# Part of a down product is moved behind the start of a mixer, and queries and key scores are made in two halves

## The chip, the cores and the metric

The kernel runs on one core of a Trainium2 chip, in f32. The metric is the device time of one execution, in microseconds; 2289.24 is the median of three (2287.36 to 2290.9).

## What is computed

256 tokens of width 1024 go through a first block (modulated SwiGLU, a mixer of sparse attention and a recurrent branch, a second SwiGLU) and then through two hybrid layers. Only these matter here:

```python
# first block, second SwiGLU
y = swiglu(h, ffn2_w_gate[l], ffn2_w_up[l], ffn2_w_down[l])       # down: 2816 -> 1024
x = x + 0.5 * m[8][:, None, :] * rmsnorm(y, ffn2_post_g[l])
# each of two hybrid layers
u = rms_norm(x, attn_norm_w) @ w_in                               # HGRN, attention, SSM
x = x + mix @ w_out
# expert layer, for each block of 128 tokens
q = (xt @ w_query).reshape(T, H, 2, PEER_HALF)                    # H = 8 heads
s = jnp.einsum('thcd,cnd->thcn', q, sub_keys)                     # 128 keys a side
sv, si = lax.top_k(s, K)                                          # K = 16
top_s, pos = lax.top_k(cand_s, K); idx = jnp.take_along_axis(cand_i, pos, axis=-1)
a = jnp.einsum('thkd,td->thk', down[ib], xb)
c = gate * jax.nn.gelu(a)
out = jnp.einsum('thk,thkd->td', c, up[ib])
```

## The kernel before

Tokens are handled in two blocks of 128 (tb 0 and 1). All dense weights are stored as 1 MB tiles (128 x 2048) and pass through a ring of four slots; SyncE issues their loads in the order of the list `STREAM` (L72), each as soon as the tile four places before it has been used (`tiles_used`, L1092). The wait for a tile and the release of its slot are part of the product that uses it.

The second SwiGLU of the first block ends with the down product `down(1, tb, 0, 11)` (L1406, L1397): 11 tiles for each token block, four products of 128 x 512 a tile, summed in PSUM banks 4 and 5 for block 0 and 6 and 7 for block 1. Its tiles are loaded once for each block. `post(2, tb)` closes it: ScalarE takes the mean square and the root (L1125 to L1128), VectorE the reciprocal, scales (L1614) and adds to x (L1615).

Then come four mixers, `i` = 0 to 3 (two layers, two token blocks). A mixer is three generators, one for each of ScalarE (L285), TensorE (L446) and VectorE (L700), whose `yield`s number its steps. `Beside(...).to(k)` runs the steps up to k. Mixer 0 runs alone, all steps in a row. Mixers 1 to 3 run beside the experts of the token block before: step k of TensorE after pick k of 128, those of the two others at slots of the same count. Steps touched by the change or the prediction:

- step 4: transposes of the normalized x (L452), copied and scaled by ScalarE (L308); steps 8 to 48: the input product (`weights`, L458), with the recurrence levels between
- step 57: logits; 58: the SSM product (L637), behind VectorE's L868; 61, 62: transposed probabilities (L617); 64, 65: values (L624)
- 68: transposes of the mix, 71 to 78: output product; 84: transposes of htok; 87 to 94: queries in two chunks (four parts each); 95, 97: transposes of the queries; 101, 103: key scores (L696), copied by ScalarE at L433, L437 and L443

The experts follow (`picks_*`, L909 to L1085). Per unit of one head, VectorE searches the 16 best keys on each side, their 16 best pairs and the indices (`search`, steps 0 to 6); it waits for both halves of the scores first. GpSimd gathers 16 pairs of rows for each token, one pick (8 KB a token, 1 MB in all) at a time, into a ring of eight slots of `wide` (L1060), slot k again once TensorE has used pick k - 8. VectorE makes dot products two picks at a time (L1011), ScalarE the gelu (L925) and the diagonals (L930), TensorE the weighted sum in banks 6 and 7 (L944). The first index of mixer 0's scores starts the first gather.

SBUF is laid out twice in the same bytes: `one` for the first block, `two` for the layers. In `one`, `actT` (the input of the down product), `rows` and `xn` lie at the front, where `wide` lies in `two`.

```python
            for tb in range(TB):
                down(1, tb, 0, 11)
            pe.wait_ge(m["smalls2_loaded"], 32)
            Beside(mixer_tensor(pe, 0, tile)).to(LAST)
            for i in range(MIXERS - 1):
                picks_tensor(pe, i, Beside(mixer_tensor(pe, i + 1, tile)))
            picks_tensor(pe, MIXERS - 1)
```

## Time and profile before

| | |
|---|---|
| median of three runs | 2289.24 us |
| profiled execution | 2289.02 us, span from the first to the last instruction 2287.3 |
| TensorE busy | 1992.7 us, 87% of the span, mean granted clock 0.963 |
| VectorE / ScalarE / GpSimd busy | 57% / 27% / 27% |
| bytes | 796.41 MB, mean 348 GB/s |
| gathers | 574.65 MB, 61.5% of the 16 DMA engines' span |
| weight tiles and other loads by sequencer | 209.73 MB, 24.5% |

Busy shares are means over the whole span. The span has two parts: up to about 800 us dense products (the first block, and mixer 0 alone), then the expert stage. A chain of waits follows the work that ended last back from the end; idle time in brackets stands before an instruction, with what ended it.

### The profile page before, as it was taken

To read this page: it belongs to the slowest core of one execution; us is meant where nothing else is said; L and a number is where in the kernel's file an instruction comes from. 1 tells how busy PE (TensorE), PEld (TensorE's weight loads), DVE (VectorE), ACT (ScalarE), POOL (GpSimd) and SP (SyncE) were. 2 spreads that over 40 slices of the span, in tenths; PEclk is the share of its full clock that TensorE was granted. 3 is DMA by queue.
4 is the path that set the end of the run, shared out by engine and by line. 5 is a ranking of instruction groups with operands and counts; after the bars stand their busy time and mean duration, and the time that the engine had idled before them with its cause. 6 is when DMAs were issued, how large, how long until landed. Compare 5 with 4: busy or idle time off the path is not lost.

```text
span 2287.3 us, 20001 instructions
## 1 busy us (share of the span) xinstructions
PE 1992.7 (87%) x6128; PEld 1070.0 (47%) x6128; DVE 1295.1 (57%) x3368; ACT 620.1 (27%) x1510; POOL 611.9 (27%) x554
## 2 busy tenths in 40 slices
PE   3999999899998769989979898977999898777776
PEld 2886577588644334444424443433444443333332
DVE  5550155200015276776577778658687767777764
ACT  2000125200013232453223245223225332222221
POOL 1100000000000043334333333334333334454442
PEclk8999999999999879999999999999999999999999
DMA  9987943444685499999999999999999999999997
GB/s 389 390 341 271 316 148 137 167 157 154 236 299 210 147 379 421 421 383 403 421 417 405 421 421 388 422 422 405 419 420 419 360 399 416 403 422 420 421 417 324
DMA packets 113380, 796.41 MB, mean 348 GB/s; under 512 B 12377, under 2 KB 15961, under 8 KB 17416
## 3 DMA queue, kind: packets, MB, share of 16 engines
q0 software_dynamic: 78912, 574.65, 61.5%
q1 hardware_dynamic: 28944, 209.73, 24.5%
q10 hardware_dynamic: 5432, 10.93, 1.3%
q8 instruction: 42, 0.69, 0.1%
q14 instruction: 50, 0.41, 0.0%
HBM read 794.19 MB, written 4.75 MB: 349 GB/s over the span
## 4 chain that ended last, share of the span: by engine, by line
PE 56%; DMA 22%; DVE 11%; ACT 5%; issue 4%; POOL 1%; POOLq 0%; DVEq 0%; ACTq 0%
DMA wide<-experts_in,pick_idx 21%; PE PS L944 17%; PE PS L1351 17%; PE PS L458 10%; PE PS L1401 8%; DVE wide L1011 4%; ACT diag L930 1%; POOL wide L1060 1%; DMA ring<-wts_in 1%; DMA early<-ada_in 1%; DVE topi L962 1%; DVE topi L959 1%; ACT L925 1%; DVE topf L961 1%; PE PS L696 1%
## 5 line engine op out<-in xcount | busy, mean ns | idle before, releaser
L944 PE MATMUL PS<-wide,diag 128*128 128x512 f32 x2048 | 994.4, 624 | 225.2 <-ACT diag L930 219.4
L1060 POOL DMA_INDIRECT wide<-experts_in,pick_idx x512 | 584.7, 1142 | 1326.3 <-PE PS L944 796.3
L1011 DVE CUSTOM_DVE_ANT_0 wide<-wide,htok 128x1024 f32<-128x1024 f32 x512 | 619.9, 1225 | 278.0 <-DMA wide<-experts_in,pick_idx 271.2
L944 PEld LDWEIGHTS PS<-wide,diag 128*128 128x128 f32 x2048 | 386.1, 197 | 751.5 <-issue 409.2
L1351 PE MATMUL PS<-hT,ring 128*128 128x256 f32 x1744 | 382.7, 382 | 15.2 <-DMA ring<-wts_in 11.6
L1351 PEld LDWEIGHTS PS<-hT,ring 128*128 128x128 f32 x1744 | 333.5, 192 | 64.5 <-issue 16.7
L458 PE MATMUL PS<-ring,hTm 128*128 128x512 f32 (+1 forms) x704 | 324.4, 591 | 2.1 <-ACT hTm L308 1.7
L930 ACT ACTIVATE diag<-cst,coef 128x128 f32<-128x128 f32 x512 | 177.6, 394 | 275.9 <-DVE coef L1022 273.4
L925 ACT ACTIVATE coef<-dots 128x2 f32<-128x2 f32 x256 | 52.3, 204 | 639.8 <-DVE dots L1011 639.3
L458 PEld LDWEIGHTS PS<-ring,hTm 128*128 128x128 f32 x704 | 134.5, 193 | 164.8 <-issue 155.5
L1401 PE MATMUL PS<-ring,actT 128*128 128x512 f32 x352 | 153.8, 598 | 2.0 <-DMA ring<-wts_in 2.0
L1636 DVE TENSOR_TENSOR actT<-silu,PS 128x256 f32<-128x256 f32 (+1 forms) x44 | 18.5, 421 | 231.8 <-ACT silu L1188 231.8
L1401 PEld LDWEIGHTS PS<-ring,actT 128*128 128x128 f32 x352 | 67.2, 192 | 86.1 <-issue 82.4
L1188 ACT ACTIVATE silu<-PS 128x256 f32<-128x256 f32 x44 | 16.9, 384 | 290.4 <-PE PS L1351 290.4
L1629 DVE CUSTOM_DVE_ANT_0 early<-early,cact 128x1024 f32<-128x1024 f32 x72 | 84.2, 1219 | 14.2 <-DMA early<-ada_in 14.1
L1612 DVE RECIPROCAL stat<-stat 128x1 f32<-128x1 f32 x6 | 1.0, 164 | 140.0 <-ACT stat L1128 140.0
L1022 DVE TENSOR_TENSOR coef<-coef,gate 128x2 f32<-128x2 f32 x256 | 41.2, 161 | 61.7 <-ACT coef L925 56.7
L925 ACT ACT_TABLE_LOAD x58 | 74.4, 1283 | 1.0
L1116 POOL TENSOR_TENSOR bias_t<-bias_t,early 128x1024 f32<-128x1024 f32 (+1 forms) x2 | 7.9, 3930 | 192.4 <-DVE early L1731 192.4
L1109 POOL DMA_DIRECT2D early<-ada_in x32 | 16.9, 528 | 132.4 <-DVE modr L1629 132.4
L1011 DVE DVE_READ_ACCUMULATOR2_ANT dots<- 128x1 f32 x512 | 41.9, 82 | 0.0
L913 ACT ACT_TABLE_LOAD x31 | 39.8, 1283 | 0.5
(316 smaller groups left out, 1241.0 us busy)
## 6 DMA issues: line engine op xcount, KB each, us to landing
ring<-wts_in SPq DMA_DIRECT2D x199, 1024.0 KB, 5.7
early<-ada_in POOLq DMA_DIRECT2D x36, 1024.0 KB, 8.5
wide<-experts_in,pick_idx POOLq DMA_INDIRECT x512, 12.4
strip_t<-strips_one ACTq DMA_DIRECT2D x1, 2048.0 KB, 12.0
strip_dil<-strips_one ACTq DMA_DIRECT2D x1, 1536.0 KB, 19.0
x<-x_in ACTq DMA_DIRECT2D x1, 1024.0 KB, 9.0
bias_t<-strip_t ACTq DMA_DIRECT2D x1, 1024.0 KB, 13.8
wrow<-norm_row_in ACTq DMA_DIRECT2D x2, 512.0 KB, 6.5
```

What stands on the lines that cost most here:

```text
L458: last = pe.matmul(PS[:, c % 2, 0:n], hTm[:, k, :], w[:, k % 4 * BANK:k % 4 * BANK + n], start=k == 0, stop=k == 7, skip_group_check=True)
L696: last = pe.matmul(PS[:, G2 + h // 2, (h % 2) * 256:(h % 2 + 1) * 256], qT[:, h * P:(h + 1) * P], o2(l, "keys", 0, 256), start=True, stop= ...
L913: act.activation(topf[:, 128 + 32 * (u % 2):144 + 32 * (u % 2)], topf[:, 112 + 32 * (u % 2):128 + 32 * (u % 2)], ACT.Exp).then_inc(m["gate ...
L925: act.activation(coef[:, 0, rr % 2, :], dots[:, rr % 2, :], ACT.Gelu_apprx_tanh).then_inc(m["gelu_ready"], 1)
L930: act.activation(diag[:, (rr * ROUND + j) % RING, :], ident, ACT.Copy, scale=coef[:, 1, rr % 2, j:j + 1])\
L944: last = pe.matmul(PS[:, ACC + half, :], diag[:, n % RING, :], ups[:, n % RING, half * BANK:(half + 1) * BANK], start=k == 0, stop=k == PI ...
L1011: v.tensor_tensor_reduce(out=downs[:, n % RING, :], in0=downs[:, n % RING, :], in1=htok[:, tb, :], scale=1.0, scalar=0.0, op0=ALU.mult, op ...
L1022: v.tensor_tensor(coef[:, 1, rr % 2, :], coef[:, 0, rr % 2, :], gate[:, u % 4, rr * ROUND:(rr + 1) * ROUND], ALU.mult)\
L1060: pool.indirect_dma_start(pairs_of_rows[:, k % RING, :, :].rearrange("p c n -> p (c n)"), None, experts.rearrange("l e d -> (l e) d"), bas ...
L1351: last = pe.matmul(outp, a, b, start=i == 0, stop=i == len(pairs) - 1)
L1401: last = pe.matmul(PS[:, bank + half, :], src[:, 2 * t + k, tb * P:(tb + 1) * P], w[:, k * D + half * BANK:k * D + (half + 1) * BANK], sta ...
L1629: v.tensor_tensor_reduce(out=w, in0=w, in1=cact[:, :], scale=1.0, scalar=0.0, op0=ALU.mult, op1=ALU.add, accum_out=modr[:, 8 * j + n:8 * j ...
```

## The change

The down product of token block 1 is no longer one piece. Three of its 11 tiles are used right behind token block 0's product; one (the fourth) after step 57 of mixer 0, the two halves of the fifth after steps 62 and 65, the sixth after step 82, and five behind the mixer's last step. `STREAM` has the tiles in the new order; their number is the same. `actT` now lies under the last three gather slots, so GpSimd waits before gather 5 of the first unit until the last of these tiles has been used. `post(2, 1)` is called in the experts of block 0, on ScalarE ahead of the first gelu, on VectorE after the first two dot products; it writes to `lgt` and `htok[:, 1]` in place of `junk` and `xn`. TensorE waits for it ahead of the first expert product.

In every mixer the second query chunk is split around the first chunk's transposes and key scores, scores of heads 0 to 3 go to banks 4 and 5 and those of heads 4 to 7 to banks 2 and 3, ScalarE's copies follow that order, and VectorE waits for the first half ahead of head 0 and for the second ahead of head 4. The arguments `beside=None, opening=None` are added to `picks_scalar` and `picks_vector`.

```diff
@@ -71,14 +71,17 @@
-          ("out1", "out1", [0, 1, 0, 1, 2, 3, 2, 3]), ("gu2", "gu2", range(FT)), ("dn2", "dn2", [*range(FT // 2)] * TB)]
-for _i in range(MIXERS):
+          ("out1", "out1", [0, 1, 0, 1, 2, 3, 2, 3]), ("gu2", "gu2", range(FT)), ("dn2", "dn2", range(FT // 2)),
+          ("late0", "dn2", range(0, 3)), ("in_0", "in_0", range(14)), ("late1", "dn2", range(3, 5)), ("out_0", "out_0", range(4)),
+          ("late2", "dn2", range(5, 6)), ("query_0", "query_0", range(4)), ("late3", "dn2", range(6, FT // 2))]
+for _i in range(1, MIXERS):
...
+LATE = [FIRST[f"late{_p}"] + _t for _p, _c in enumerate((3, 2, 1, 5)) for _t in range(_c)]
@@ -159,8 +162,7 @@
-        actT = sb("actT", [P, FT, S], stack=one)
-        rows = sb("rows", [P, 3, D], stack=one)
+        row1 = sb("row1", [P, D], stack=one)
@@ -181,10 +183,15 @@
+        used = D + 2 * D + KC * S + 4 * S + W1 + WC1 + 16 * 3 + 8 + 72 * 2 + 24 * 2 + 16 + 8 + 32
+        sb("low_rest", [P, RING * 2 * D - 3 * 2 * D - used], stack=one)
+        actT = sb("actT", [P, FT, S], stack=one)
+        sb("high_rest", [P, 3 * 2 * D - FT * S], stack=one)
...
+        row0 = sb("row0", [P, D], stack=one)
+        cact = sb("cact", [P, D], stack=one)
...
-        cact = sb("cact", [P, D], stack=one)
@@ -203,6 +210,7 @@
+        rows = [row0[:, :], row1[:, :], htok[:, 1, :]]
@@ -428,19 +436,17 @@
             for c in range(2):
-                yield 92 + 4 * c
+                yield 92 + 10 * c
                 act.wait_ge(m["tiles_used"], FIRST[f"query_{i}"] + 2 * c + 2)
                 act.copy(u[:, c * BANK:(c + 1) * BANK], PS[:, c, :]).then_inc(m["q_copied"], 1)
-            yield 99
-            for b in (0, 1):
-                act.wait_ge(m["q_T"], 2 * i + b + 1)
-                act.copy(u[:, D + b * BANK:D + (b + 1) * BANK], PS[:, G2 + b, :]).then_inc(m["qT_copied"], 1)
-            for b in (0, 1):
-                yield 104 + b
-                act.wait_ge(m["scores_ready"], 2 * i + b + 1)
+                yield 96 + 10 * c
+                act.wait_ge(m["q_T"], 2 * i + c + 1)
+                act.copy(u[:, D + c * BANK:D + (c + 1) * BANK], PS[:, G2 + c, :]).then_inc(m["qT_copied"], 1)
+                yield 100 + 10 * c
+                act.wait_ge(m["scores_ready"], 2 * i + c + 1)
                 if i:
                     act.wait_ge(m["topk_ready"], EXPERT_HEADS * i)
-                act.copy(key_scores.rearrange("p h c n -> p (h c n)")[:, b * D:(b + 1) * D], flat(PS[:, G2 + 2 * b:G2 + 2 * b + 2, :]))\
+                act.copy(key_scores.rearrange("p h c n -> p (h c n)")[:, c * D:(c + 1) * D], flat(PS[:, 4 - 2 * c:6 - 2 * c, :]))\
                     .then_inc(m["s_copied"], 1)
@@ -681,21 +687,35 @@
             weights("query", 0, 3)
-            for part in range(4):
-                yield 91 + part
-                weights("query", 1, part)
-            for c in range(2):
-                yield 95 + 2 * c
+            qT = u[:, D:2 * D]
+
+            def query_turn(c):
                 pe.wait_ge(m["q_copied"], 2 * i + c + 1)
                 turn(G2 + c, u[:, c * BANK:(c + 1) * BANK], 4).then_inc(m["q_T"], 1)
-            qT = u[:, D:2 * D]
-            for b in (0, 1):
-                yield 101 + 2 * b
-                pe.wait_ge(m["qT_copied"], 2 * i + 2)
+
+            def keys(b):
+                pe.wait_ge(m["qT_copied"], 2 * i + b + 1)
                 for h in range(4 * b, 4 * b + 4):
-                    last = pe.matmul(PS[:, G2 + h // 2, (h % 2) * 256:(h % 2 + 1) * 256], qT[:, h * P:(h + 1) * P],
+                    last = pe.matmul(PS[:, 4 - 2 * b + (h - 4 * b) // 2, (h % 2) * 256:(h % 2 + 1) * 256], qT[:, h * P:(h + 1) * P],
                                      o2(l, "keys", 0, 256), start=True, stop=True)
                 last.then_inc(m["scores_ready"], 1)
+
+            yield 91
+            weights("query", 1, 0)
+            yield 94
+            query_turn(0)
+            yield 95
+            weights("query", 1, 1)
+            yield 98
+            keys(0)
+            yield 99
+            weights("query", 1, 2)
+            yield 100
+            weights("query", 1, 3)
+            yield 104
+            query_turn(1)
+            yield 107
+            keys(1)
@@ -919,6 +939,8 @@
+                if u == 0:
+                    opening()
@@ -964,8 +986,8 @@
                 if step == 0:
-                    if h == 0:
-                        v.wait_ge(m["s_copied"], 2 * (g // EXPERT_HEADS) + 2)
+                    if h % 4 == 0:
+                        v.wait_ge(m["s_copied"], 2 * (g // EXPERT_HEADS) + 1 + h // 4)
                     best16(best[:, 0:16], besti[:, 0:16], key_scores[:, h, 0, :])
@@ -1036,6 +1058,8 @@
+                    if u == rr == 0:
+                        opening()
@@ -1070,6 +1094,8 @@
                         pool.wait_ge(m["ups_used"], u * K16 + k - RING + 1)
+                    if opening and k == RING - 3:
+                        pool.wait_ge(m["tiles_used"], LATE[-1] + 1)
                     pool.sem_inc(m["gather_starts"], 1)
@@ -1122,8 +1148,8 @@
-            def mean_square(src, n, col, width, done):
-                act.activation(junk[:, 0:n], src, ACT.Square, accum_out=stat[:, col:col + 1]).then_inc(m["sq_done"], 1)
+            def mean_square(src, n, col, width, done, out=junk):
+                act.activation(out[:, 0:n], src, ACT.Square, accum_out=stat[:, col:col + 1]).then_inc(m["sq_done"], 1)
@@ -1135,7 +1161,8 @@
                 act.wait_ge(m["tiles_used"], done)
-                mean_square(flat(PS[:, bank:bank + 2, :]), D, 12 + 4 * i + 2 * tb, D, "y_root_fb")
+                mean_square(flat(PS[:, bank:bank + 2, :]), D, 12 + 4 * i + 2 * tb, D, "y_root_fb",
+                            flat(lgt) if i == 2 and tb else junk)
@@ -1148,7 +1175,7 @@
-                act.copy(rows[:, i, :], flat(PS[:, bank:bank + 2, :])).then_inc(m["rows_ready"], 1)
+                act.copy(rows[i], flat(PS[:, bank:bank + 2, :])).then_inc(m["rows_ready"], 1)
@@ -1329,12 +1356,9 @@
-            first = Beside(mixer_scalar(act, 0))
-            first.to(1)
-            post(2, 1, FIRST["dn2"] + 22, 6)
-            first.to(LAST)
+            Beside(mixer_scalar(act, 0)).to(LAST)
...
-                picks_scalar(act, i, Beside(mixer_scalar(act, i + 1)))
+                picks_scalar(act, i, Beside(mixer_scalar(act, i + 1)), lambda: post(2, 1, LATE[-1] + 1, 6))
@@ -1587,10 +1611,33 @@
             pe.wait_ge(m["rows_ready"], 3)
-            for tb in range(TB):
-                down(1, tb, 0, 11)
+            down(1, 0, 0, 11)
+
+            def late(t, halves=(0, 1)):
+                w = tile(LATE[t])
+                for k in halves:
+                    for half in range(2):
+                        last = pe.matmul(PS[:, 6 + half, :], actT[:, 2 * t + k, P:S], w[:, k * D + half * BANK:k * D + (half + 1) * BANK],
+                                         start=t == k == 0, stop=t == 10 and k == 1, skip_group_check=True)
+                if 1 in halves:
+                    last.then_inc(m["tiles_used"], 1)
+
+            for t in range(3):
+                late(t)
             pe.wait_ge(m["smalls2_loaded"], 32)
-            Beside(mixer_tensor(pe, 0, tile)).to(LAST)
+            first = Beside(mixer_tensor(pe, 0, tile))
+            first.to(57)
+            late(3)
+            first.to(62)
+            late(4, (0,))
+            first.to(65)
+            late(4, (1,))
+            first.to(82)
+            late(5)
+            first.to(LAST)
+            for t in range(6, 11):
+                late(t)
+            pe.wait_ge(m["x_ready"], 6)
             for i in range(MIXERS - 1):
@@ -1611,8 +1658,9 @@
-                V(v.scalar_tensor_tensor(xn[:, tb, :], flat(PS[:, bank:bank + 2, :]), r, rows[:, i, :], ALU.mult, ALU.mult))
-                v.tensor_tensor(x[:, tb, :], x[:, tb, :], xn[:, tb, :], ALU.add).then_inc(m["x_ready"], 1)
+                y = rows[2] if i == 2 and tb else xn[:, tb, :]
+                V(v.scalar_tensor_tensor(y, flat(PS[:, bank:bank + 2, :]), r, rows[i], ALU.mult, ALU.mult))
+                v.tensor_tensor(x[:, tb, :], x[:, tb, :], y, ALU.add).then_inc(m["x_ready"], 1)
@@ -1806,12 +1854,9 @@
-            first = Beside(mixer_vector(v, V, 0))
-            first.to(3)
-            post(2, 1, 6)
-            first.to(LAST)
+            Beside(mixer_vector(v, V, 0)).to(LAST)
...
-                picks_vector(v, V, i, Beside(mixer_vector(v, V, i + 1)))
+                picks_vector(v, V, i, Beside(mixer_vector(v, V, i + 1)), lambda: post(2, 1, 6))
```

## Rows read from the trace of the kernel before

**Rows 1.** The page, section 2: GB/s of DMA in 40 slices of 57.2 us.

```profile
GB/s 389 390 341 271 316 148 137 167 157 154 236 299 210 147 379 421 421 383 403 421 417 405 421 421 388 422 422 405 419 420 419 360 399 416 403 422 420 421 417 324
```

**Rows 2.** Stretches: us, engines busy (instructions), PEclk, DMA share, GB/s.

```profile
806.00:814.00 8.00, 0.00 (x0) 0.00 (x0) 6.49 (x21) 1.70 (x3) 5.87 (x6) 0.50 0.98 378
820.00:2260.00 1440.00, 1245.16 (x3208) 550.49 (x3207) 1029.57 (x2743) 469.30 (x1172) 574.66 (x502) 0.97 1.00 412
840.00:870.00 30.00, 30.00 (x80) 13.53 (x79) 17.13 (x42) 10.53 (x22) 8.91 (x9) 0.99 1.02 423
```

**Rows 3.** Chain that ended last: start us, us, what.

```profile
594.44 75.55 PE PS L1401 x176
```

**Rows 4.** Timeline of TensorE: start us, us, line op, tiles, count [idle before].

```profile
669.81 1.04 PE L452 MATMUL PS<-cst,mx 128*128 128x128 f32 x8
672.54 12.28 PE L458 MATMUL PS<-ring,hTm 128*128 128x512 f32 x28 [1.69 <-ACT hTm L308]
...
723.54 1.00 PE L570 MATMUL PS<-i_tok,u 128*128 128x64 f32 x8
...
737.10 2.82 PE L637 MATMUL PS<-xdt,u 128*128 128x64 f32 x12 [3.13 <-DVE u L868]
...
744.08 1.97 PE L624 MATMUL PS<-v_tok,hTm 128*128 128x64 f32 x8 [2.16 <-ACT hTm L410]
...
747.85 1.97 PE L452 MATMUL PS<-cst,mx 128*128 128x128 f32 x8 [0.94 <-DVE mx L895]
750.19 14.84 PE L458 MATMUL PS<-ring,hTm 128*128 128x512 f32 x32 [0.38 <-ACT hTm L418]
768.91 1.94 PE L452 MATMUL PS<-cst,htok 128*128 128x128 f32 x8 [3.88 <-DVE htok L906]
770.72 14.80 PE L458 MATMUL PS<-ring,hTm 128*128 128x512 f32 x32
...
787.53 3.73 PE L696 MATMUL PS<-s,u 128*128 128x256 f32 x16 [0.68 <-ACT u L437]
815.64 11.09 PE L944 MATMUL PS<-wide,diag 128*128 128x512 f32 x20 [24.38 <-ACT diag L930]
```

**Rows 5.** Stretches of the first mixer and its clock; columns as in rows 2.

```profile
735.00:751.00 16.00, 9.94 (x39) 8.27 (x40) 5.00 (x15) 8.52 (x32) 0.00 (x0) 0.50 0.00 1
753.00:768.00 15.00, 12.03 (x29) 4.99 (x27) 1.97 (x4) 1.44 (x3) 0.00 (x0) 1.00 0.74 247
769.00:772.00 3.00, 3.00 (x10) 2.24 (x11) 0.00 (x0) 1.17 (x2) 0.00 (x0) 0.50 0.05 22
```

**Rows 6.** Timeline of ScalarE, the norm of block 0 and two copies.

```profile
632.25 1.02 ACT L1126 ACTIVATE silu<-PS 128x1024 f32<-128x1024 f32 x1 [37.38 <-PE PS L1401]
...
633.38 1.28 ACT L1128 ACT_TABLE_LOAD   x1
634.67 0.29 ACT L1128 ACTIVATE stat<-stat,cst 128x1 f32<-128x1 f32 x1
...
778.69 0.59 ACT L433 COPY u<-PS 128x512 f32<-128x512 f32 x1 [7.22 <-PE PS L458]
...
791.29 1.01 ACT L443 COPY key_scores<-PS 128x1024 f32<-128x1024 f32 x1 [0.72 <-PE PS L696]
```

**Rows 7.** Timeline of VectorE, the norm's rest, mx, the first search step.

```profile
635.20 1.28 DVE L1614 SCALAR_TENSOR_TENSOR xn<-PS,stat,rows 128x1024 f32<-128x1024 f32 x1
636.52 1.23 DVE L1615 TENSOR_TENSOR x<-x,xn 128x1024 f32<-128x1024 f32 x1
...
640.17 0.75 DVE L715 TENSOR_SCALAR mx<-x,mst 128x1024 f32<-128x1024 f32 x1 [0.25 <-DVE mst L714]
...
792.34 0.29 DVE L958 MAX8 topf<-key_scores 128x8 f32<-128x128 f32 x1 [23.48 <-ACT key_scores L443]
```

**Rows 8.** Timeline of GpSimd: the first gather issued.

```profile
803.43 0.99 POOL L1060 DMA_INDIRECT wide<-experts_in,pick_idx  x1 [450.10 <-DVE pick_idx L997]
```

**Rows 9.** Who line 443 (score copies, four mixers) waited for: us, times.

```profile
  PE PS L696: 4.5, 4
```

More of the change, by code:

```diff
@@ L907, in mixer_vector, with picks_scalar @@
                 .then_inc(m["h_ready"], 1)
-        def picks_scalar(act, i, beside=None):
+        def picks_scalar(act, i, beside=None, opening=None):
             def exps(u):
@@ L948, in picks_tensor, with picks_vector @@
                     beside.to(k)
-        def picks_vector(v, V, i, beside=None):
+        def picks_vector(v, V, i, beside=None, opening=None):
             iota = C("iota")
```

## The prediction

> **What bounds the kernel now.** I read the page's slices first. The bytes moved per second are low in slices 11 to 14 (572 to 800 us) and at a plateau from slice 16 on, with a few dips [rows 1]. The stretches behind it say the same: from 820 to 2260 us the DMA share is 1.00 at 412 GB/s [rows 2]. So the expert stage is a stage of bytes: 512 gathers of 1 MB, and the weight tiles of three more mixers beside them. At the 421 GB/s of its undisturbed slices a tile or a gather (128 x 2048 x 4 B) takes 2.49 us. What is done before the first gather has no such cover: it is one chain through TensorE and the small steps between engines. A microsecond taken out of it moves the whole expert stage forward, and a megabyte that is pushed behind the first gather costs 2.49 us again. The chain of waits puts the whole second-block down product on it: 176 matmul instructions in 75.55 us, 0.429 us each [rows 3]. A tile is eight instructions (two products of two halves, and one f32 matmul shows as two), so 3.43 us. The first token block's product ends at 594.44 + 88 x 0.429 = 632.2 us, the second's at 670.0. Then the first mixer runs alone, with TensorE waiting at four places near its end [rows 4], and from 791.3 to 815.6 us TensorE has nothing at all [rows 4].
>
> **1. Eight of eleven tiles leave the front.** Three stay ahead of the mixer: 632.2 + 24 x 0.429 = 642.5 us, where the mixer's first transposes stood at 669.8 [rows 4]. Their input, the normalized x of token block 0, is there earlier: VectorE has written mx by 640.9 [rows 7]. The loads hide: these are the same 22 tile loads in another order, the ring is fed four tiles ahead, and no idle stretch of TensorE in the down product or in the mixer names the ring. **-27.5 us.**
>
> **2. The closing norm of block 1 leaves the mixer's beginning.** ScalarE ran its square and root there ahead of the scaled copies of the transposes, and TensorE sat idle for 1.69 us [rows 4]. Without it the first copy starts behind the first four transposes (half of 1.04 us), about 0.9 us sooner. **-0.9 us.** The norm runs later instead (6).
>
> **3. Tiles put into the mixer.** Each costs what it is longer than the wait that it fills, at full clock: a tile of 3.43 us into 3.13 us (before L637), +0.3; half a tile of 1.72 into 2.16 (before L624), 0; half a tile into 0.94 (before the mix transposes), +0.8; a tile of 3.43 into 3.88 (before the htok transposes), 0 [rows 4]. **+1.1 us.** If a cover is shorter by the time it is reached, the difference is added, at most 3.4 us for a tile.
>
> **4. The clock.** TensorE is at 0.50 from 735 to 751 us and from 769 to 772 us, both times after such a wait, and at 1.00 between [rows 5]. The work on the chain in these stretches is slow: twelve 64-column instructions of L637 take 2.82 us where eight of the same form take 1.00 us at full clock, those of L624 2.97, the two groups of eight transposes 1.97 and 1.94 where the first group takes 1.04, and the 32 weight products behind each 14.84 and 14.80 where 32 x 0.429 is 13.7 [rows 4]. Were all of it at full clock, the chain would shorten by 1.4 + 1.4 + 0.5 + 1.1 + 0.5 + 0.9 = 5.8 us. The change puts dense matmuls into just these waits, but ScalarE and VectorE steps still leave TensorE partly idle between 738 and 748, so I take most of it, **-4.5 us**, with bounds 0 and -5.8, and a worse case in the rivals. The Trainium skill ("TensorE: Matmul & The Clock Gate", Part 1) says that the throttled state is the default and that activity releases it. By that rule an inserted tile can also begin throttled. Rows 5 agree with the rule, and show no inserted tile.
>
> Steps 1 to 4: **-31.8 us** for the end of the first query chunk, which ScalarE copied at 778.69 [rows 6].
>
> **5. Queries and keys in halves.** Now the search starts at 792.34, 13.65 us behind that copy, after the second chunk (6.9 us), both turns, all keys (3.73) and both score copies [rows 4, 6, 7]. In the new order it needs one query part (1.72, covering the 0.59 copy), one turn (0.5), a second part (1.72, covering the next copy), half the keys (1.87), one score copy (1.01), and some 0.3 of handing over: 7.1 us. **-6.6 us**, so the search begins 38.4 us earlier. The index search for head 0 stays as it is, so the first gather is issued 11.1 us behind that start, as now [rows 7, 8]. The new wait of VectorE, for the second half of the scores at head 4, is hidden by two units of expert work.
>
> **6. What is late next.** The DMA engines start on gathers some 2 us behind the first issue [rows 8], so at 766.8 instead of 805.2. But before, the ring had been filled with four tiles of the next mixer by then. Now five late tiles of the down product stand between, so these four loads are released one by one as the late tiles are used, beside the first gathers: 4 x 2.49 = **+10.0 us** of bytes. It would be free only if the stage had slack in its bytes, and from 840 to 870 us it has none, at 423 GB/s [rows 2]. The ramp that the first gathers show now, 378 GB/s for 8 us instead of 421, is filled by the tiles: **-0.8 us** [rows 2]. The new wait of GpSimd, before gather 5, ends with the last late tile. That is at 778.7 - 31.8 + 12.9 (three query parts, two turns, the keys and their copies) + 17.2 (five tiles) = 777.0 us. Gathers 5 to 15 and all later ones are queued behind it. The queue doesn't run dry: nine megabytes (gathers 0 to 4 and four tiles) last until about 789.
>
> The deferred norm waits for the same tile. Behind it on ScalarE stand the gelu and the diagonals of expert 0, on VectorE the weighing of round 0, and TensorE waits for its sum because banks 6 and 7 are shared. By its rows: square and its read 1.2, table load 1.28, root 0.29, reciprocal 0.16, scale 1.28, add 1.23, and handing over, 5.9 us, so x is ready at 782.9 [rows 6, 7]. A search step and the weighing follow, and the first expert product starts at about 785.1, against 815.64 [rows 4]: -30.5. So TensorE would allow 30.5, the bytes 38.4 - 10.0 + 0.8 = 29.2. The smaller one counts.
>
> **7. Later mixers.** The same reordering stands in mixers 1 to 3, beside picks. I cost it at nothing: bytes bound there, and the score copies waited for the keys by 4.5 us over all four mixers [rows 9]. If that cover goes, each mixer loses some of it; bounds -1 and +3 us for the three.
>
> **Sum.** -27.5 - 0.9 + 1.1 - 4.5 - 6.6 + 10.0 - 0.8 = **-29.2 us**. The profiled execution took 2289.02 (span 2287.3), 0.2 below the median of 2289.24; so 2259.8, rounded **2260 us**. Its own range, by the bounds of 4 and 7 and some 2 us for the queues of 6: 2254 to 2267.
>
> **Rivals.**
> *Throttled insertions.* The tiles in the waits run at 1.2 GHz, 6.9 us a tile, and lengthen what they were to fill. For: 0.50 stands in rows 5 in exactly these waits. Against: the clock was still 1.00 when the first wait began, and it came back soon in the dense products behind it. Price: no clock gain (+4.5), first tile +3.4, halves of the second +1.3 and +1.7: 10.9 us, so 2271.
> *The tile bytes cost nothing.* If the expert stage at its beginning is paced by TensorE and not by bytes (it is busy all through 840 to 870 us [rows 2], with expert products and mixer weights), and the deferred norm is quicker than I think, up to the whole head start stays: 2289.0 - 38.4 = 2251.
> *Slower.* In mixers 1 to 3 ScalarE now stops for TensorE at slots 101, 107 and 111, ahead of the gelus in its queue. If TensorE lags two picks with mixer work (2 x 3.43 = 6.9 us) at two more of these stops, with nothing queued to cover them, three mixers lose 41 us: 2301. It decides from 29.2 / 3 = 9.7 us a mixer on. Against: 4.5 us in all now [rows 9], and eight gathers in the ring.
> *It doesn't do what it says.* The gate before gather 5 leaves DMA dry for what was won: within 5 us of 2289. It would take 29 dry us, where I count nine megabytes queued.
>
> **How the numbers follow.** Forecast 0.64; throttled insertions 0.15; bytes for nothing 0.15; slower 0.04; no effect 0.02. To hold 8 in 10 the range takes the forecast's own, the throttled case at 2271 and most of the way to 2251: 2251 to 2271. Faster by over 0.2% (4.6 us, about what a measurement of this kernel can tell from no change) 0.94, within 0.02, slower 0.04.
>
> **What would show it.** In the changed profile: mixer transposes at 642.5; first search step near 754 and first gather issued near 765; last late tile near 777; first expert product near 785; granted clock above 0.50 in most of 707 to 720 (the former 735 to 751); DMA at the plateau from 768 on, without a gap near 790; the expert stage from the first gather to the end longer by about 9 us. A search start later than 760 makes the first steps wrong; a first product before 785 with an end later than 2265 makes 7 wrong; an end below 2254 makes the price of the four tiles wrong.

## The result and the profile after

The changed kernel took 2257.61 us in the median of four runs (2253.47 to 2260.71), against 2290.07 for the kernel before: a ratio of 0.9859 with a 95% interval of 0.9836 to 0.9881, 32.5 us less (27 to 38). The forecast was 2260. The profiled execution took 2254.79 us, its span 2253.1. It was already 2.2 us ahead at the end of block 0's down product (ScalarE's square begins at 630.05, in rows 6 at 632.25), which nothing in the change touches. So I count all that follows from that square, in every profile.

The slices of bytes after, of the same page section as rows 1: slice 14 (a slice is 56.3 us now) has 310 in place of 147, and the plateau is as before.

```profile
GB/s 389 381 353 262 316 171 150 164 153 149 218 283 217 310 421 421 421 367 422 422 419 421 416 422 382 422 421 390 422 409 411 370 414 419 417 421 418 412 412 331
```

The chain that ended last, from the down product to the first expert product (start us, us, what):

```profile
592.25 37.77 PE PS L1425 x88
630.01 10.30 PE PS L1620 x24
640.79 1.15 ACT hTm L316 x4
641.98 12.28 PE PS L464 x28
...
703.41 3.63 PE PS L1620 x8
707.04 1.30 PE PS L643 x12
...
712.48 1.55 PE PS L630 x12
714.03 1.77 PE PS L1620 x4
...
717.47 14.02 PE PS L464 x32
...
735.35 1.09 PE PS L458 x8
...
756.87 17.18 PE PS L1620 x40
774.07 1.11 ACT lgt L1152 x2
...
777.02 1.29 DVE htok L1662
778.34 1.23 DVE x L1663
781.58 6.38 PE PS L966 x8
```

Read beside rows 3 and 4: 24 late instructions stand ahead of the mixer instead of 88; ScalarE's copies follow the first transposes at once, without the square and root between; the tile at 703.41 fills the former 3.13 us, and the twelve instructions behind it (L643, formerly L637) take 1.30 us of the chain. In the timeline, the view of rows 4, they take 1.45, where rows 4 have 2.82. Clock and bytes in stretches like those of rows 2 and 5 (us, engines busy, PEclk, DMA share, GB/s):

```profile
705.00:721.00 16.00, 13.62 (x59) 7.84 (x58) 5.00 (x15) 8.12 (x30) 0.00 (x0) 1.00 0.39 133
722.00:738.00 16.00, 15.27 (x42) 6.92 (x41) 2.82 (x4) 2.52 (x5) 0.00 (x0) 1.00 0.88 303
763.00:796.00 33.00, 24.13 (x56) 10.60 (x55) 20.46 (x51) 10.78 (x20) 11.18 (x12) 0.84 1.01 419
```

The clock is 1.00 where it was 0.50, and the DMA engines are full from the first gathers on. ScalarE's copy of the first query chunk, VectorE's first search step, and GpSimd's gathers 0, 4, 5 and 8:

```profile
743.87 0.58 ACT L441 COPY u<-PS 128x512 f32<-128x512 f32 x1 [6.75 <-PE PS L464]
```

```profile
750.51 0.29 DVE L980 MAX8 topf<-key_scores 128x8 f32<-128x128 f32 x1 [15.22 <-ACT key_scores L449]
```

```profile
761.61 0.99 POOL L1084 DMA_INDIRECT wide<-experts_in,pick_idx  x1 [407.52 <-DVE pick_idx L1019]
...
766.64 0.94 POOL L1084 DMA_INDIRECT wide<-experts_in,pick_idx  x1 [0.30 <-issue]
774.85 0.94 POOL L1084 DMA_INDIRECT wide<-experts_in,pick_idx  x1 [7.27 <-PE PS L1620]
...
786.14 0.99 POOL L1084 DMA_INDIRECT wide<-experts_in,pick_idx  x1 [7.88 <-PE PS L966]
```

Gather 5 waits 7.27 us for the last late tile, gather 8 for the first expert product. In the window from 763 to 796 neither shows in the DMA share.

**The head start along the experts.** Each profile has 512 dot products of VectorE (L1011 before, L1033 after). The table is the start of dot product k, less the start of the square named above, minus the same in the kernel before; so it is the head start in us at that point, and the last column that at the end of the span. For instance k = 8, after and before: 798.01 - 630.05 and 829.89 - 632.25, so -29.7.

```profile
798.01 1.23 DVE L1033 CUSTOM_DVE_ANT_0 wide<-wide,htok 128x1024 f32<-128x1024 f32 x1 [0.50 <-DMA wide<-experts_in,pick_idx]
```

```profile
829.89 1.23 DVE L1011 CUSTOM_DVE_ANT_0 wide<-wide,htok 128x1024 f32<-128x1024 f32 x1 [0.52 <-DMA wide<-experts_in,pick_idx]
```

| profile | first search step | first expert product | k = 8 | 56 | 128 | 352 | 416 | end |
|---|---|---|---|---|---|---|---|---|
| changed kernel | -39.6 | -31.9 | -29.7 | -30.4 | -30.5 | -28.3 | -32.2 | -32.0 |
| again (e5) | -39.6 | -31.9 | -29.3 | -29.7 | -27.7 | -26.7 | -29.9 | -29.6 |
| a third time (e12) | -39.6 | -31.9 | -30.0 | -29.9 | -29.4 | -29.1 | -33.6 | -33.6 |
| e1, halves only | -7.2 | -7.0 | -7.0 | -7.7 | -6.6 | -8.0 | -12.7 | -12.5 |
| e2, move only | -32.6 | -27.4 | -28.7 | -28.8 | -27.4 | -27.7 | -28.1 | -28.2 |
| e3, five tiles without bytes | -39.6 | -31.9 | -35.0 | -33.9 | -30.4 | -32.3 | -36.1 | -36.1 |
| e4, two tile-times more | -39.6 | -25.0 | -28.1 | -27.8 | -26.6 | -27.8 | -30.9 | -31.0 |
| e10, four tile-times more | -39.6 | -18.1 | -21.3 | -21.3 | -22.1 | -21.2 | -24.6 | -24.6 |
| e6, halves in mixer 0 only | -39.6 | -31.9 | -29.6 | -30.3 | -27.5 | -27.3 | -27.7 | -27.6 |
| e7, inserts ahead | -24.5 | -16.7 | -14.8 | -15.1 | -13.6 | -15.2 | -17.9 | -17.9 |
| e8, inserts behind | -34.8 | -13.3 | -15.7 | -16.5 | -15.7 | -14.3 | -18.0 | -18.1 |
| e9, six tiles | -39.6 | -36.3 | -38.6 | -39.7 | -37.8 | -40.2 | -43.2 | -44.1 |
| e11, finer pieces | -40.5 | -34.0 | -34.2 | -34.2 | -31.5 | -31.2 | -35.4 | -35.1 |

Up to the first expert product the same kernel gives the same number to 0.1 us. Beside the experts it doesn't: three profiles of the changed kernel lie 2.8 apart at 128 and 4.0 at the end. Its 13 timed runs of all groups go from 2251.75 to 2262.62, median 2258.44, and the runs of the kernel before from 2282.43 to 2291.68. The table's first two columns are therefore firm, and a difference of less than some 3 us further right isn't, by one profile.

### The profile page after: what moved, and what is told of

It reads as the page before. It is cut to its first block, busy times and chain, and to the rows that moved or that the text cites. A ratio compares the mean times of both kernels' runs of the same rounds, so it can differ in the third digit from the quotient of the medians.

```text
span 2253.1 us, 20003 instructions
## 1 busy us (share of the span) xinstructions
PE 1997.4 (89%) x6128; PEld 1071.9 (48%) x6128; DVE 1294.5 (57%) x3368; ACT 621.3 (28%) x1511; POOL 623.2 (28%) x554
## 4 chain that ended last, share of the span: by engine, by line
PE 54%; DMA 25%; DVE 11%; ACT 4%; issue 4%; POOL 2%; POOLq 0%; DVEq 0%; ACTq 0%
DMA wide<-experts_in,pick_idx 23%; PE PS L1375 17%; PE PS L966 16%; PE PS L464 10%; PE PS L1425 6%; DVE wide L1033 4%; POOL wide L1084 2%; PE PS L1620 1%; ACT diag L952 1%; DMA ring<-wts_in 1%; DMA early<-ada_in 1%; DVE topi L981 1%; DVE topi L984 1%; PE PS L477 1%; PE PS L1464 1%
## 5 line engine op out<-in xcount | busy, mean ns | idle before, releaser
L966 PE MATMUL PS<-wide,diag 128*128 128x512 f32 x2048 | 1004.6, 630 | 194.2 <-ACT diag L952 188.6
L1084 POOL DMA_INDIRECT wide<-experts_in,pick_idx x512 | 595.9, 1164 | 1280.1 <-PE PS L966 780.3
L1033 DVE CUSTOM_DVE_ANT_0 wide<-wide,htok 128x1024 f32<-128x1024 f32 x512 | 619.8, 1224 | 285.4 <-DMA wide<-experts_in,pick_idx 279.3
L966 PEld LDWEIGHTS PS<-wide,diag 128*128 128x128 f32 x2048 | 390.9, 199 | 723.3 <-issue 425.0
L1425 PE MATMUL PS<-ring,actT 128*128 128x512 f32 x264 | 115.9, 600 | 2.0 <-DMA ring<-wts_in 2.0
L1425 PEld LDWEIGHTS PS<-ring,actT 128*128 128x128 f32 x264 | 50.4, 192 | 64.9 <-issue 61.3
L1033 DVE DVE_READ_ACCUMULATOR2_ANT dots<- 128x1 f32 x512 | 42.1, 82 | 0.0
## 6 DMA issues: line engine op xcount, KB each, us to landing
bias_t<-strip_t ACTq DMA_DIRECT2D x1, 1024.0 KB, 13.6
```

The lines of the kernel that those rows point to most:

```text
L966: last = pe.matmul(PS[:, ACC + half, :], diag[:, n % RING, :], ups[:, n % RING, half * BANK:(half + 1) * BANK], start=k == 0, stop=k == PI ...
L1033: v.tensor_tensor_reduce(out=downs[:, n % RING, :], in0=downs[:, n % RING, :], in1=htok[:, tb, :], scale=1.0, scalar=0.0, op0=ALU.mult, op ...
L1084: pool.indirect_dma_start(pairs_of_rows[:, k % RING, :, :].rearrange("p c n -> p (c n)"), None, experts.rearrange("l e d -> (l e) d"), bas ...
L1425: last = pe.matmul(PS[:, bank + half, :], src[:, 2 * t + k, tb * P:(tb + 1) * P], w[:, k * D + half * BANK:k * D + (half + 1) * BANK], sta ...
```

## Experiments

Two theories went into them. B: behind the first gather the end follows the bytes that are still to be moved, as the prediction's smaller figure says. P: it follows the first expert product. Their runs of the kernel before are 2287.84 us in the median for e1 to e4, 2288.05 for e5 to e8, and 2286.62 for e9 to e12.

**e1: halves only.** The diff's hunks for the queries, keys, score copies and the search's wait, on the kernel before.

```diff
-                    if h == 0:
-                        v.wait_ge(m["s_copied"], 2 * (g // EXPERT_HEADS) + 2)
+                    if h % 4 == 0:
+                        v.wait_ge(m["s_copied"], 2 * (g // EXPERT_HEADS) + 1 + h // 4)
```

> The kernel before with the queries and keys in halves alone; the down product stays whole. Theory B (bytes: from the first gather on the end moves with the start of the gathers plus the megabytes that are still to be loaded): the search starts 6.6 us earlier, so does the first gather, the four tiles of the next mixer are loaded by then as before, so the end comes 6.6 us earlier, 2283.5 against 2290. Theory P (the end moves with the first expert product on TensorE): the same 6.6, as the first product follows the first dot products. Either fails if the end moves by less than 3.

2279.33 us, ratio 0.9967 (0.9954 to 0.9980): 7.6 us less by the ratio (5 to 11), 8.5 by the medians. The search starts 7.2 us earlier, 0.6 more than worked out. The end gains more than that in the profile, 12.5 (the profiled execution was the fastest of five), and the table says where: 4.7 us come between dot products 352 and 416.

**e2: move only.** The changed kernel with the old order of queries and keys.

```diff
-                    if h % 4 == 0:
-                        v.wait_ge(m["s_copied"], 2 * (g // EXPERT_HEADS) + 1 + h // 4)
+                    if h == 0:
+                        v.wait_ge(m["s_copied"], 2 * (g // EXPERT_HEADS) + 2)
```

> The changed kernel with the old order of queries and keys; only the down product is moved. The search starts 31.8 to 33 us earlier than before. Theory B: the last late tile ends at about the same time as in the changed kernel, but the gathers start 6.6 later, so about two of the next mixer's four tiles are loaded before the first gather and only two are paid behind it (5 us): 26 to 27 us faster than before, 2263.5. Theory P: the first expert product waits for the norm behind the last late tile in both, so it moves by 1 us at most against the changed kernel: 30 to 31 faster than before, 2259.5.

2264.49 us, ratio 0.9899 (0.9884 to 0.9914): 23.1 us less by the ratio (20 to 27), 23.4 by the medians. The search gains 32.6. P is too high by 7 us; B's 26 to 27 is just at the interval's end. The first product is 4.4 us later than in the changed kernel, not 1: its first two dot products come 7 us later, and VectorE's part of the norm stands behind them. Both expectations had that wrong. So e2 refutes P's figure, and not yet P: with the first product where it was (-27.4), P too would give an end near the measured one.

**e3: the last five tiles without their bytes.**

```diff
-          ("late2", "dn2", range(5, 6)), ("query_0", "query_0", range(4)), ("late3", "dn2", range(6, FT // 2))]
+          ("late2", "dn2", range(5, 6)), ("query_0", "query_0", range(4))]
...
-                w = tile(LATE[t])
+                w = tile(LATE[t]) if t < 6 else None
...
-                        last = pe.matmul(PS[:, 6 + half, :], actT[:, 2 * t + k, P:S], w[:, k * D + half * BANK:k * D + (half + 1) * BANK],
+                        last = pe.matmul(PS[:, 6 + half, :], actT[:, 2 * t + k, P:S], w[:, k * D + half * BANK:k * D + (half + 1) * BANK] if w is not None else masks,
```

> The changed kernel with the last five tiles of the down product multiplied by constants that lie in SBUF: the same 40 matmul instructions, gate and norm, but five tile loads fewer, so the ring holds the next mixer's four tiles before the first gather. This part of the product is left out of the result. Theory B: 10 us of bytes go, of which some 4 are given back because gather 8 waits for the first product: 6 us faster than the changed kernel, 2251.5, and the ninth and tenth dot products come 5 to 6 us earlier than in the changed kernel against the end of block 0's down product. Theory P: the first product doesn't move, so the end doesn't: within 1.5 us of 2257.6.

2257.43 us, ratio 0.9872 (0.9858 to 0.9887): no faster than the changed kernel (30.4 us less than before, where the changed kernel's three groups gave 32.5, 32.9 and 26.9). But the ninth dot product is 5.3 us earlier, just what B said. This is where the next bound stands: the first expert product, at -31.9 in both, frees the slot of the gather that dot product 8 needs. In e3 the DMA engines are no longer full from 765 to 800 us (share 0.89), least of all around gather 8, which is issued at 788.73 (0.57):

```profile
765.00:800.00 35.00, 27.45 (x65) 12.18 (x64) 25.70 (x71) 14.06 (x32) 12.67 (x14) 0.85 0.89 331
787.00:791.00 4.00, 4.00 (x8) 1.65 (x7) 2.58 (x7) 2.16 (x4) 0.99 (x1) 0.64 0.57 205
```

Of the 5.3 us, 3.9 are left at 56 and 1.2 at 128, against the mean of the changed kernel's three profiles. The same picks, 56 to 80, in e3, in the changed kernel and in e6 (below), which loads the tiles as the changed kernel does:

```profile
953.19:1027.04 73.85, 64.20 (x186) 32.18 (x187) 52.95 (x152) 31.30 (x79) 26.21 (x23) 0.93 0.91 352
```

```profile
954.13:1025.54 71.41, 62.51 (x186) 30.99 (x187) 53.00 (x151) 31.27 (x79) 25.64 (x23) 0.95 0.98 378
```

```profile
959.17:1033.05 73.88, 64.21 (x186) 32.06 (x187) 52.97 (x151) 31.30 (x79) 24.90 (x23) 0.93 0.94 363
```

In e3 the DMA engines idle by 9% of 74 us, in the changed kernel by 2% of 71, and it is tempting to say that the saved bytes are lost in this stretch, beside mixer 1's attention steps. The third row forbids it: e6 has saved no byte and takes as long as e3, with the same lower clock, and e3 stays 3.6 us ahead of it from 56 to 80. e9 (below), which has saved the same bytes and is at -39.7, takes 71.4 us like the changed kernel. Further on, e3 is ahead of the mean again, by 4.3 us at 352 and 4.4 at the end, while its median shows nothing. Its four runs spread by 7 us and the changed kernel's thirteen by 11, so they speak against the 10 us that the prediction charges for these bytes, and can't exclude a gain of some 3 us. At their own place the four tiles cost 5.3 us that the first product allows to be seen; how much of that lasts to the end is not shown.

**e4 and e10: two and four tile-times more for TensorE, no bytes**, behind the last late tile; e10 has `range(8)` in place of `range(4)`.

```diff
             for t in range(6, 11):
                 late(t)
+            for t in range(4):
+                for half in range(2):
+                    last = pe.matmul(PS[:, 6 + half, :], actT[:, t, P:S], masks, start=False, stop=t == 3, skip_group_check=True)
+            last.then_inc(m["late_done"], 1)
```

> The changed kernel with two more tile-times of TensorE work (16 instructions on constants, no loads) behind the last late tile, ahead of the gate, the norm and the first expert product: all three come 6.9 us later. The result is changed by these products. Theory B: nine megabytes are queued, the DMA engines stay busy until the first product frees slots, so 0 to 2 us slower than the changed kernel, 2257.6 to 2259.6. Theory P: the end moves with the first product, 6.9 us slower, 2264.5.

> Four more tile-times of TensorE work behind the last late tile (e4 had two), no loads; the result is changed by these products. The gate, the norm and the first expert product come 13.7 us later than in the changed kernel. Theory M: the slack against the bytes, 2 to 4 us, is used up and the rest counts: 10 to 12 us slower than the changed kernel at dot product 128 and at the end, about 2266. Theory A: at most 5 us slower at the end.

e4: 2257.09 us, ratio 0.9871 (0.9856 to 0.9885), no slower than the changed kernel, with the first product 6.9 us later. P alone falls. e10: 2265.95 us, ratio 0.9907 (0.9891 to 0.9923): 6.3 us slower than the changed kernel's 2259.70 in the same group, 7.5 slower than the median of all its runs (2258.44), with the first product 13.7 us later. At dot product 128 the two stand 2.6 and 7.1 us behind the mean of the changed kernel's three profiles. So the slack between the first product and the bytes is 4 to 7 us, not 2 to 4. Dot product 8 says it most sharply. In e3, e4 and e10 its head start is that of the first product plus 3.1, 3.1 and 3.2 us: the product bounds it. In the changed kernel that bound would be at -35.0, and the bytes hold dot product 8 at -29.7 (the mean of three), 5.3 us later. Both bounds are real there, and the later one counts. The DMA engines show it, from 770 to 796 us in e4 and from 765 to 800 in e10:

```profile
770.00:796.00 26.00, 18.45 (x38) 7.73 (x37) 11.30 (x24) 9.87 (x17) 3.54 (x4) 0.81 1.01 423
```

```profile
765.00:800.00 35.00, 27.46 (x61) 11.91 (x60) 13.91 (x33) 8.58 (x14) 5.62 (x6) 0.88 0.90 362
```

**e5 and e12: the changed kernel again.**

> The changed kernel once more, as the reference of this group and a second profile of it. All theories: 31 to 33 us faster than before in the median. In the first profile it stood 30.5 us ahead of before at dot product 128 (both counted from the end of block 0's down product) and 32 at the end. If the difference of the two numbers belongs to the kernel it comes again; if it is chance among executions it can have either sign, within some 4 us.

> The changed kernel as the reference of this group, and a third profile. All theories: 31 to 34 us faster than before in the median; its lead over before at dot product 8 is again 29.3 to 29.7 us, and between dot products 16 and 128 it differs from the other two profiles by up to 3 us.

2255.11 us, ratio 0.9849 (0.9834 to 0.9865), and 2259.70 us, ratio 0.9881 (0.9862 to 0.9899). Two groups of the same kernel, on two chips, are 4.6 us apart; this is the scale against which a few microseconds between groups are to be read.

**e6: the halves in mixer 0 only**, old order in mixers 1 to 3.

```diff
-            for c in range(2):
-                yield 92 + 10 * c
+            if i == 0:
+                for c in range(2):
+                    yield 92 + 10 * c
...
+            else:
+                for c in range(2):
+                    yield 92 + 4 * c
```

> The changed kernel with the halves in mixer 0 alone; mixers 1 to 3, which run beside the experts, have the old order of queries and keys. Theory N (the prediction's step 7: nothing): within 1.5 us of the changed kernel. Theory O (the new order shortens the handover from one token block's experts to the next): 2 to 4 us slower than the changed kernel in the median, with the same lead at dot product 64. The slower rival of the prediction would show as faster by more than 2.

2257.93 us, ratio 0.9864 (0.9847 to 0.9882), 2.8 us above e5 of its group. The medians alone would not carry it. The profiles do: between dot products 352 and 416 all eleven profiles with the new order in mixer 3 gain 2.7 to 4.7 us on the kernel before, and the two with the old order (e2, e6) 0.4. Picks 352 to 364, where mixer 3's queries and keys stand, in before, e6 and the changed kernel:

```profile
1871.81:1904.21 32.40, 32.40 (x91) 16.20 (x90) 18.53 (x43) 12.33 (x28) 14.75 (x13) 1.00 0.97 371
```

```profile
1847.27:1879.65 32.38, 32.38 (x91) 16.27 (x90) 18.57 (x44) 12.32 (x28) 15.25 (x13) 1.00 0.98 373
```

```profile
1841.32:1870.55 29.23, 29.23 (x80) 14.08 (x79) 18.74 (x44) 11.02 (x27) 14.58 (x12) 1.00 1.00 409
```

TensorE is busy without a gap in all three. With the old order the bytes come at 371 and 373 GB/s, below the plateau, so there TensorE is the bound; with the new order they are near the plateau again (409 GB/s). With the query parts, turns and keys spread over later steps these twelve picks hold fewer of its instructions (80 instead of 91) and take 3.2 us less. (In the second profile, e5, only 1.4 us come here and 1.8 more by dot product 416.) Mixers 1 and 2 show no such gain: at dot product 352, behind them, e6 (-27.3) lies within the spread of the changed kernel's three profiles. Why they don't is open.

**e7 and e8: the three inserted tiles ahead of the mixer, or behind the keys.**

```diff
-            first.to(57)
-            late(3)
-            first.to(62)
-            late(4, (0,))
-            first.to(65)
-            late(4, (1,))
-            first.to(82)
-            late(5)
```

> The three tiles that stand in the mixer's waits moved ahead of the mixer: six ahead, five behind, none inside. Theory C (the inserted tiles also hold the clock up): the waits are empty again, the clock falls to 0.50 in them, and the chain to the search grows by 10.3 - 1.1 + 4.5 = 13.7 us; end 13 to 14 us later than the changed kernel, about 2270. Theory W (they only fill waits, the clock would be up anyway): 9.2 us, about 2266. The granted clock between the logits and the mix transposes tells.

> The same three tiles moved behind the keys: three ahead, eight behind. The search starts only 3.4 us later than in the changed kernel (clock +4.5, no overshoot -1.1), the last late tile and the first expert product 13.7 later. By bytes alone (three more tiles are loaded behind the first gather) +3.4 + 7.5 = 10.9 us; by the first product 13.7; the larger one counts by the prediction's rule: 2268 to 2271. If only the start of the gathers counted, 2261.

e7: 2272.52 us, ratio 0.9924 (0.9908 to 0.9940). The search starts 15.1 us later than in the changed kernel, beyond even theory C's 13.7. The waits have their low clock again:

```profile
719.00:734.00 15.00, 9.16 (x39) 7.80 (x39) 5.00 (x15) 7.15 (x27) 0.00 (x0) 0.50 0.00 1
```

```profile
720.52 2.82 PE L643 MATMUL PS<-xdt,u 128*128 128x64 f32 x12 [3.13 <-DVE u L888]
...
733.97 15.06 PE L464 MATMUL PS<-ring,hTm 128*128 128x512 f32 x32 [0.38 <-ACT hTm L426]
```

e8: 2271.85 us, ratio 0.9929 (0.9912 to 0.9946). The search starts 4.9 us later only, but the last late tile ends 18.6 later: three tiles (10.3), that 4.9, and two waits of 1.3 us for loads between the last late tiles. The end moves with the later one, less the slack: 13.6 us in the profile.

**e9: six tiles, five left out altogether.**

```diff
-            for t in range(6, 11):
-                late(t)
```

> The changed kernel without the last five tiles of the down product, neither loads nor products; this part of the product is left out. Without their bytes alone (e3) nothing was won. Theory M (two bounds, bytes and the first expert product, and the later one counts): now both go, the first product comes 7.8 us earlier than in the changed kernel and the bytes are 10 fewer, so the end comes 7 to 8 us earlier, about 2247 against 2255. Theory A (something later in the expert stage absorbs any head start beyond the changed kernel's): within 2 us of the changed kernel.

2245.80 us, ratio 0.9815 (0.9800 to 0.9830), 12.6 us below the changed kernel's 2258.44. Theory A falls: the expert stage doesn't swallow a head start in which bytes and first product move together. The first product itself is only 4.5 us earlier, as the first dot products wait for their gathers, but with the bytes gone too dot product 8 is 8.9 earlier, and 8.6 are left at 128 against the mean of the three profiles; at the end of the profile it is 12.4.

**e11: finer pieces.** The late products one by one (0.86 us each) in the waits that are left.

```diff
+            late(11)
...
+            for step, pieces in ((4, 1), (56, 1), (57, 4), (61, 1), (62, 3), (65, 2), (68, 1), (82, 4), (100, 1), (104, 1)):
+                first.to(step)
+                late(pieces)
+            first.to(LAST)
+            late(44 - at[0])
```

> The changed kernel with the late tiles cut into single products of 0.86 us, placed in the waits that its profile still shows: one behind the first transposes, one more tile in all in the waits of steps 56 to 69, two products ahead of the second half's transposes and keys. The search starts 0.5 us earlier, the last late tile and the first expert product 5 us, and one tile less is loaded behind the first gather. Theory M: 3 us faster than the changed kernel at dot product 16 (bytes 0.5 + 2.5), 3 to 5 at the end, about 2251. Theory A: no difference at the end.

2254.19 us, ratio 0.9854 (0.9834 to 0.9873), against 2259.70 and 0.9881 (0.9862 to 0.9899) for the changed kernel in its group. The first search step is 0.9 us earlier and the last late tile 6.0, but the first product 2.1, where I had expected 5: the gathers of the first two picks now come last, and the norm's VectorE part behind them. The profile is 4.5 us ahead at dot product 8, 2.3 at 128 and 3.4 at the end, against the mean of three. The intervals overlap, and runs of other groups lie as low; it is likely the best version here, and not shown to be.

## Why the prediction was right, step by step

**Steps 1 to 5, the chain to the search:** -38.4 us forecast, -39.6 measured, in three profiles alike. The mixer's transposes begin 27.5 us earlier by the common count (640.15 against 669.81), as forecast. ScalarE's copy of the first query chunk, at 743.87 against 778.69 [rows 6], is 32.6 us earlier, 31.8 forecast. With the inserted tiles TensorE's clock stays at 1.00 up to the search, and the chain from the first input product to that copy takes 101.9 us where it took 106.2: 4.3 us less, where steps 3 and 4 make 3.4. So step 4 was nearer its bound of -5.8 than the -4.5 taken, if step 3 cost its 1.1; no run separates the two. e7 and e8 price both together: without the inserted tiles the chain is 4.9 us longer beside the 10.3 of the tiles themselves. That the clock is lost without them was worked out from rows 5, and both runs show it (0.50 in 719 to 734 us of e7). The rule of the Trainium skill ("TensorE: Matmul & The Clock Gate", Part 1), that activity releases a throttled state, agrees with rows 5 (0.50 in the waits, 1.00 in the dense products from 753 us on). Of the two things it allowed, the tiles kept the clock (1.00 in both rows above) and none began throttled. Step 5: -6.6 forecast, -7.2 in e1 and -7.0 between e2 and the changed kernel.

**Step 6, what is late next:** the last late tile ended at 774.0; 777.0 was forecast, 774.8 less the 2.2 of the common start; the first product at -31.9, -30.5 forecast. Dot product 8 stands at -29.3 to -30.0, the sum's -29.2. The order of the two bounds was right: the bytes hold this dot product, and e7, with the same bytes and a search 15.1 us later, stands 14.9 us behind. But the second bound was mis-sized. The prediction lets TensorE allow 30.5 us, 1.3 more than the bytes; measured at dot product 8 it allows 35.0, 5.3 more (e3, with e4 and e10 in line). Of the price of the four tiles, +10.0, that lets 5.3 be seen; the rest is not measured, as the first product then bounds. "The smaller one counts" explains all three cases: the first product may come 7 us later for nothing that the median shows (e4), the bytes alone bring only what the first product allows (e3), and with both the end comes 12 us earlier (e9). The prediction also carries the tiles' price to the end of the stage unchanged, by a row of 30 us. That is not confirmed: e3's profile ends 4.4 us ahead, and its median not at all.

**Step 7, later mixers:** mis-sized. I cost it at nothing, with bounds -1 and +3; in mixer 3 it brings about 3 us, outside these bounds. "Bytes bound there" was wrong for the twelve picks beside the queries and keys, where in the old order TensorE is busy without a gap at 371 GB/s. With it the end of the changed kernel is at -32.0, -29.6 and -33.6, on average 2.5 below the figure at dot product 128. That is what the forecast of -29.2 lacked, and the measured 32.5 (27 to 38) doesn't contradict either number. That the sum came within 4 us of the median is in part luck: two groups of the same kernel differ by more.

**The rivals.** Throttled insertions: refuted by the clock. Bytes for nothing: refuted at dot product 8, where they cost 5.3 us. Whether the end pays for them is open (e3). Without them the stage still doesn't keep the 38.4 us, as the first product holds dot product 8 at -35.0. Slower by stops in mixers 1 to 3: the reverse happened. Dry DMA at the gate: not in the changed kernel. It begins when the first product comes 13.7 us later (e10: share 0.90) or the tiles' bytes are gone (e3: 0.89).

**Open:** what makes executions of one kernel differ by some 10 us, in the profiles beside the experts (4.0 us among three) or ahead of the change (the square begins between 630.05 and 635.45 us in the same three); why e9's 8.6 us at dot product 128 become 12.4 at the end; and how e3 can end its profile 4 us ahead of the mean and its median not at all. The last two are of the size of the spread. Open too is whether four tiles' bytes ahead of a gate cost anything at the end; more profiles of e3 and of the changed kernel side by side would tell.

## What to carry to other kernels

Work that another stage doesn't need at once can be taken apart and put into the waits of a chain; it pays twice where it also holds TensorE's clock up (here 10.3 us of tiles moved, and 4.9 us of faster steps by e7 and e8). Where a stage starts behind two bounds, work out both and the distance between them: a saving in one is worth at most that distance (here 5.3 us at dot product 8), and a delay of the other costs nothing below it. Before explaining a loss by a stretch where the DMA share falls, look at the same stretch in a run without the cause. Compare profiles from a common event, the last one that is the same in both kernels, and take more than one profile before explaining 3 us.

## What the chip showed beyond what was expected

Two stretches of one kernel reproduce very differently: the chain of one engine after another repeats to 0.1 us over three profiles (first search step 120.46, 120.46 and 120.47 us behind the square), while with 16 DMA engines full and three engines working beside them the same program spreads by 2.8 us within 128 picks.
